# mLSTM scores of heads 1 to 3 from high and low parts, in three float32r products

## The chip, the cores and the metric

The program runs on one core of a Trainium2 chip. The metric is the device time of one execution in microseconds. The time before is 1564.88 us, the median of three runs (1564.79 to 1565.66).

## The reference

Two layers of a hybrid backbone over 512 latent and 256 context tokens of width 1024, all in float32. The even layer projects its input, runs a convolution group beside a bidirectional mLSTM group (4 heads of 128), and projects out; the odd layer has pooling and attention. A ConvFFN follows in each. The part that matters here is the chunkwise mLSTM:

```
s   = einsum('bhld,bhsd->bhls', qj, kj) * exp(dmat - m_t)
num = w_inter * einsum(qj, C) + einsum('bhls,bhse->bhle', s, vj)
den = w_inter * einsum(qj, n) + sum(s, -1)
h   = num / max(abs(den), exp(-m_t))
```

It is run forward and backward with separate gates, and the two results are added. q and k are used in full float32. The kernel computes the same without a carried state: all scores of a head, weighted by one exponential for each direction.

## The kernel before, in words

The layout puts channels on the 128 partitions and tokens on the free axis (T = 768: 512 latent, then 256 context). `qkov` holds 16 blocks of 128x768: queries of heads 0 to 3, keys of heads 0 to 3, values, and the output gates. `h_hi` and `h_lo` hold the two float32r parts of the layer's input (eight blocks of 128x768 each), which are not needed once the even projection is done; later they take the parts of the mixer's output.

The mLSTM stage works through the list `ITEMS` (L193): six score items ("S", head, q) for each head, q going over the key tiles in the order 4, 5, 0, 1, 2, 3 (`ORDER`, context tiles first), and from head 1 on one item "X" for the head before, which turns its normalised result. Each engine runs its own loop over the list, and semaphores couple them:

- PE (L1029): the score of item z goes to one of two PSUM slots. It waits until DVE has read the slot two items back. Then PE weighs the item before: probabilities times values (`weigh`, L1006), into PSUM sums of the head. So each score stands ahead of the weighing of its predecessor. Before the first weighing of a head, PE waits until the sums of the head before were read (`sums_taken_fwd`, `sums_taken_rev`).
- ACT (L1584): the exponentials of an item (`exps`, two or four, with four buffers that `p_used` frees), the squares of the head before at q 1 and 2, its square root at q 3 (two table loads), and the first two exponentials of the next head at q 5, then the copy of the reverse sums.
- POOL (L2595): a triangular mask on the diagonal block of each exponential.
- DVE (L2284): score times exponential (`weighted`, L2216), and in head 0 three reciprocals for the convolution's norm, in later heads the reverse sums, the norm factors, the convolution's norm; at the end of a head the merge of the head before, the first two products of the next head and `forward_sums` (L2230), which takes the denominators and reads the sums.

The order of the work on every engine is written out by hand in these loops. The score is one plain float32 matmul for each segment (L1045), with segments 0:512 and, for context tiles, also 512:768. Elsewhere in the kernel (L741, L790, L1166) a product is three float32r matmuls of parts: high x high, high x low, low x high. A high part is an ACT copy with rounding to float32r, a low part a DVE subtraction. `vt` (L1757) is the helper for every DVE tensor_tensor, so its instructions all have that line.

Of the kernel before, what the change touches and what calls it, by code (L numbers as in the profile page):

```python
# [28 lines left out]
F32 = mybir.dt.float32  # L29
F32R = mybir.dt.float32r  # L30
ALU = mybir.AluOpType
ACT = mybir.ActivationFunctionType
AX = mybir.AxisListType

P = 128
# [4 lines left out]
T = LAT + CTX  # L40
# [6 lines left out]
HEADS = 4  # L47
# [117 lines left out]
ORDER = (4, 5, 0, 1, 2, 3)  # L165
# [34 lines left out]
def build(nc, a, out):  # L200
# [3 lines left out]
    with ctx:  # L204
        used = {}

        def sem(name):
            if name not in used:
                used[name] = ctx.enter_context(nc.semaphore(name))
            return used[name]  # L210
# [6 lines left out]
        def place(name, shape, dt=F32, offset=None):  # L217

            size = int(np.prod(shape[1:])) * (2 if dt == mybir.dt.bfloat16 else 4)
            if offset is None:  # L220
                offset = at[0]
                at[0] += (size + 31) // 32 * 32
                assert at[0] <= top, (name, at[0] - top)
            assert offset + size <= top, name
            return nc.alloc_sbuf_tensor_at(name, shape, dt, offset=offset)
# [3 lines left out]
        h_hi = place("h_hi", [P, KD, T], F32R)  # L229
# [28 lines left out]


        qkov = place("qkov", [P, 16, T], offset=A0)  # L260
        negM = place("negM", [P, 2, 2, T], offset=A0 + 8 * T * 4)
        sig_b = place("sig_b", [P, 4, T], offset=A0 + 8 * T * 4)
        v_tok = place("v_tok", [P, NT, HEADS, VW], offset=A0 + 49152)
# [612 lines left out]
        def _(pe):  # L876
# [152 lines left out]
            for z, (kind, hd, q) in enumerate(ITEMS):  # L1029
                if z == 1:  # L1030
                    weigh(*pending)
                    pending = None
                if z >= 2:
                    was, of, q_ = ITEMS[z - 2]
                    if was == "S":
                        pe.wait_ge(sem("p_ready"), 16 * of + STEPS[q_][-1][0] + 1)
                    else:
                        pe.wait_ge(sem("merged_ready"), of + 1)
                elif not z:
                    pe.wait_ge(sem("conv_centred"), 4)  # L1040
                else:
                    pe.wait_ge(sem("ln_rooted"), 1)
                if kind == "S":
                    for t0, t1 in (SEGS[T] if ORDER[q] >= NL else SEGS[LAT]):
                        last = nc.tensor.matmul(acc[:, 1, z % 2, t0:t1], qkov[:, 4 + hd, ORDER[q] * P:(ORDER[q] + 1) * P],  # L1045
                                                qkov[:, hd, t0:t1], start=True, stop=True)
                else:
                    pe.wait_ge(sem("hn_ready"), hd + 1)
                    for j in range(NT):
                        last = transpose(acc[:, 1, z % 2, j * P:(j + 1) * P], h_tok[:, j, :])  # L1050
                last.then_inc(sem("slot_full"), 1)
                if kind == "S" and pending:
                    if pending[1] == 0 and hd:
                        pe.wait_ge(sem("sums_taken_fwd"), hd)
                        pe.wait_ge(sem("sums_taken_rev"), hd)
                    weigh(*pending)
                if kind == "S":
                    pending = (hd, q)
                if not z:
                    pe.wait_ge(sem("ln_sq_summed"), 1)  # L1060
                    for t0, t1 in SEGS[T]:
                        last = nc.tensor.matmul(acc[:, 1, 1, t0:t1], ones[:, :], ln_sq[0][:, t0:t1], start=True, stop=True)
                    last.then_inc(sem("ln_var"), 1)
                    psum_free(pe, U["mlstm"] + 1)
                if (kind, hd, q) == ("S", 0, 2):
                    last_columns()
# [180 lines left out]
        def _(act):  # L1247
# [11 lines left out]
            def unit_high(n, i=0):  # L1259

                take_high(n, i)
                take_high(n + 1, i)
# [316 lines left out]
            def head_out(hd):  # L1579

                act.wait_ge(sem("merged_ready"), hd + 1)
                nc.scalar.activation(h_hi[:, 4 + hd, :], merged[hd][:, :], ACT.Copy).then_inc(sem("mix_high"), 1)

            for kind, hd, q in ITEMS:  # L1584
                if kind == "S":
                    if hd or q:
                        exps(hd, q, 2 if not q else 0, 4)
                    if hd >= 2 and not q:
                        head_out(hd - 2)
                    if (hd, q) == (0, 0):  # L1590
                        conv_root()
                    if (hd, q) == (0, 1):
                        unit_high(G["o"] + 4)
                    if q in (1, 2) and hd:
                        head_squares(hd - 1, 3 * q - 3, 3 * q)
                    if q == 3 and hd:
                        head_root(hd - 1)
                    if q == 5:
                        if hd < HEADS - 1:
                            exps(hd + 1, 0, 0, 2)  # L1600
                        else:
                            conv_silu(0)
                        act.wait_ge(sem("den_read"), hd + 1)
                        nc.scalar.activation(h_rev[:, :, :].rearrange("p (b c) t -> p b c t", b=2), head_sums_of(1), ACT.Copy
                                             ).then_inc(sem("sums_taken_rev"), 1)
                        if hd == HEADS - 1:
                            head_out(hd - 1)
# [144 lines left out]
        def _(dve):  # L1752
# [3 lines left out]
            def vt(out_, in0, in1, op):  # L1756
                return nc.vector.tensor_tensor(out_, in0, in1, op)  # L1757

            def ada_sums(c, of, i=0, first=0, end=KD):

                seq, nv = c.seq, len(c.vectors)

                def used(k):
                    return 4 * seq + 5 + k // 2 + 4 * c.per_seq * i

                for k in range(first, end):
                    if k % 2 == 0:
                        dve.wait_ge(ada_full[k // 2], 16 * (seq + 1) + 16 * c.per_seq * i)
                    for e, x_ in enumerate(c.vectors):
                        w, scale = ada_w[:, k // 2, k % 2, :], cond[:, k, x_:x_ + 1]  # L1770
                        if not k:
                            ins = nc.vector.tensor_scalar(of[e], w, scale, None, ALU.mult)
                        else:
                            if k % 2 == 0:
                                dve.wait_ge(ada_used, used(k - 1))
                            else:
                                sd.wait(sd.value() - (nv - 1))
                            ins = nc.vector.scalar_tensor_tensor(of[e], w, scale, of[e], ALU.mult, ALU.add)
                        if k % 2 and e == nv - 1:
                            ins.then_inc(ada_used, 1)  # L1780
                        else:
                            sd.done(ins)
# [492 lines left out]
            def head_end(z, hd):  # L2275
# [3 lines left out]
                    weighted(z + 1, hd + 1, 0, 0, 2)  # L2279
                forward_sums(hd)  # L2280

            beside = [Chunk((0, 1), BESIDE["out0"][0] + e, 0, 0, 0) for e in range(2)]
            sums_e = sums_beside["out0"]
            for z, (kind, hd, q) in enumerate(ITEMS):  # L2284
                dve.wait_ge(sem("slot_full"), z + 1)
                if kind == "X":
                    nc.vector.scalar_tensor_tensor(merged[hd][:, :], acc[:, 1, z % 2, 0:T], vec0[:, 88 + hd:89 + hd],
                                                   qkov[:, 12 + hd, :], ALU.mult, ALU.mult).then_inc(sem("merged_ready"), 1)
                    head_end(z, hd + 1)
                    continue  # L2290
                weighted(z, hd, q, 2 if hd and not q else 0, 4)
                if hd == 0 and q in (2, 3, 4):
                    conv_inverse(256 * (q - 2))
                if (hd, q) == (0, 1):
                    unit_low(28)
                if q == 0 and hd:
                    reverse_sums(hd - 1)
                if q == 1 and hd >= 2:
                    head_low(hd - 2)
                if q == 2 and hd:  # L2300
                    head_inverse(hd - 1)
                if q == 4 and hd:
                    head_normed(hd - 1)
                if hd in (1, 2) and q in (2, 3):
                    conv_normed(2 * (hd - 1) + q - 2)
                if hd == HEADS - 1 and q in (1, 3):
                    ada_sums(beside[0], sums_e[0], first=q // 2, end=q // 2 + 1)
                if q == 5 and not hd:
                    head_end(z, hd)

# [345 lines left out]
```

## Time and profile before

| | |
|---|---|
| median of three runs | 1564.88 us |
| profiled execution, its own time | 1565.75 us |
| its span | 1564.0 us |
| granted TensorE clock | 0.999 |
| busy in the span: PE, PEld, DVE, ACT, POOL | 99%, 85%, 67%, 37%, 2% |
| mLSTM stage | first score at 269.70 us, first product of the output projection at 344.31 us |

The spans are microseconds from the start of one profiled execution. A busy PE is not a PE at its peak: matmuls overlap, so the time that one holds the engine is read from its start to the next one's start. A bracket behind an instruction tells how long its engine was idle before it and what ended that.

### The profile page before, as it was taken

How to read it: one execution, taken by the hardware profiler on the slowest of the kernel's cores; microseconds unless marked ns; L12 is line 12 of the kernel's file. 1: busy time of each engine (PE TensorE's matmuls, PEld its weight loads, DVE VectorE, ACT ScalarE, POOL GpSimd, SP SyncE). 2: the span in 40 equal slices, each digit the busy share in tenths (PEclk: the TensorE clock that was granted, in tenths of full speed). 3: DMA queues.
4: the chain of work that ended last, by engine and by line, in shares of the span. 5: the costliest groups of instructions: out<-in, count | busy, mean ns of one | idle time of the engine just before them, and what ended most of it. 6: DMA issues, size and time to landing. Idle time of an engine off the chain costs nothing. (4 is left out here: it accounts for less than half of the span.)

```text
span 1564.0 us, 21770 instructions
## 1 busy us (share of the span) xinstructions
PE 1544.2 (99%) x8590; PEld 1325.1 (85%) x8590; DVE 1047.2 (67%) x1567; ACT 572.4 (37%) x870; POOL 24.3 (2%) x66
## 2 busy tenths in 40 slices
PE   8999999999999999999999999998999999999998
PEld 5888888778898888888888888988988888888887
DVE  4999999888848784678626446877647543444346
ACT  5423224684722221122211225635646332322233
POOL 0000000220000000000000000000000000000000
PEclk9999999999999999999999999999999999999999
DMA  9632132125136453445333223340022323233232
GB/s 323 198 80 81 55 109 67 68 83 147 34 111 220 161 189 121 149 162 195 113 100 129 55 91 71 107 140 28 1 68 68 95 93 117 72 107 108 81 99 89
DMA packets 132746, 171.54 MB, mean 110 GB/s; under 512 B 16114, under 2 KB 88498, under 8 KB 132666
## 3 DMA queue, kind: packets, MB, share of 16 engines
q1 hardware_dynamic: 131770, 168.25, 33.7%
q0 software_dynamic: 640, 2.10, 0.3%
q8 instruction: 55, 0.90, 0.2%
q14 instruction: 25, 0.20, 0.0%
q10 hardware_dynamic: 256, 0.08, 0.0%
HBM read 166.17 MB, written 2.15 MB: 108 GB/s over the span
## 5 line engine op out<-in xcount | busy, mean ns | idle before, releaser
L741 PE MATMUL acc<-h_hi,w_hi 128*128 128x512 f32 (+1 forms) x1424 | 494.5, 351 | 0.0
L741 PE MATMUL acc<-h_lo,w_hi 128*128 128x512 f32 (+1 forms) x1424 | 492.4, 349 | 0.0
L741 PE MATMUL acc<-h_hi,w_lo 128*128 128x512 f32 (+1 forms) x1424 | 492.3, 349 | 0.0
L1757 DVE TENSOR_TENSOR w_lo<-raw,w_hi 128x1024 fp32r<-128x1024 f32 x183 | 218.1, 1219 | 131.9 <-ACT w_hi L1257 131.7
L741 PEld LDWEIGHTS acc<-h_hi,w_lo 128*128 128x128 f32 x1424 | 267.1, 189 | 35.0
L741 PEld LDWEIGHTS acc<-h_hi,w_hi 128*128 128x128 f32 x1424 | 267.3, 189 | 34.5
L741 PEld LDWEIGHTS acc<-h_lo,w_hi 128*128 128x128 f32 x1424 | 267.2, 189 | 33.8
L1257 ACT ACTIVATE w_hi<-raw 128x1024 fp32r<-128x1024 f32 x183 | 186.5, 1053 | 216.3 <-PE acc L790 150.7
L790 PE MATMUL acc<-w_hi,hid_hi 128*128 128x512 f32 x434 | 169.5, 391 | 0.0
L790 PE MATMUL acc<-w_hi,hid_lo 128*128 128x512 f32 x434 | 168.9, 389 | 0.0
L790 PE MATMUL acc<-w_lo,hid_hi 128*128 128x512 f32 x434 | 168.8, 389 | 0.0
L1633 ACT ACTIVATE gpad<-acc 128x1024 f32<-128x1024 f32 (+1 forms) x33 | 28.0, 885 | 211.2 <-PE acc L700 95.6
L2386 DVE TENSOR_SCALAR hid<-gpad,ffn_cw 128x512 f32 (+1 forms) x66 | 25.2, 438 | 112.0 <-ACT gpad L1633 111.6
L790 PEld LDWEIGHTS acc<-w_hi,hid_lo 128*128 128x128 f32 x434 | 81.5, 188 | 17.1
L790 PEld LDWEIGHTS acc<-w_lo,hid_hi 128*128 128x128 f32 x434 | 81.5, 188 | 16.7
L790 PEld LDWEIGHTS acc<-w_hi,hid_hi 128*128 128x128 f32 x434 | 81.5, 188 | 16.6
L2130 DVE SCALAR_TENSOR_TENSOR conv_u<-conv_u,dw_w 128x783 f32<-128x783 f32 x90 | 88.2, 1026 | 0.0
L1643 ACT ACTIVATE hid_hi<-hid (+2 forms) x22 | 28.0, 1274 | 145.1 <-DVE hid L1757 145.1
L2384 DVE SCALAR_TENSOR_TENSOR hid<-gpad,ffn_cw,hid 128x512 f32 (+3 forms) x132 | 77.5, 656 | 0.0
L1757 DVE TENSOR_TENSOR hid<-hid,acc 128x1024 f32 (+3 forms) x22 | 32.7, 1487 | 52.4 <-PE acc L741 51.8
L790 PE MATMUL acc<-w_hi,h_hi 128*128 128x512 f32 x160 | 63.5, 397 | 0.0
L790 PE MATMUL acc<-w_hi,h_lo 128*128 128x512 f32 x160 | 62.4, 390 | 0.0
(300 smaller groups left out, 2067.8 us busy)
## 6 DMA issues: line engine op xcount, KB each, us to landing
ada_w<-in_ada_w SPq DMA_DIRECT2D x96, 512.0 KB, 5.7
raw<-in_ffn_w_in SPq DMA_DIRECT2D x88, 512.0 KB, 3.6
raw<-in_ffn_w_out SPq DMA_DIRECT2D x44, 512.0 KB, 4.4
raw<-in_even_w_in SPq DMA_DIRECT2D x24, 512.0 KB, 4.5
ada<-in_ada_w SPq DMA_DIRECT2D x8, 1024.0 KB, 12.0
raw<-in_odd_w_in SPq DMA_DIRECT2D x12, 512.0 KB, 3.7
raw<-in_even_w_out SPq DMA_DIRECT2D x8, 512.0 KB, 5.9
raw<-in_odd_w_out SPq DMA_DIRECT2D x8, 512.0 KB, 4.0
```

The source lines that it names most:

```text
L741: last = nc.tensor.matmul(acc[:, s, m, t0:t1], w[:, slot, kk, c], x_[:, k, t0:t1], start=(k == 0 and q == 0), stop=(k == KD - 1 and q == 2))
L790: last = nc.tensor.matmul(tile_bank(name, a, j), x_[:, k, j * P:(j + 1) * P], w[:, m_ % 4, 2 * kk:2 * kk + 2, :].rearrange("p a c -> p (a ...
L1257: nc.scalar.activation(dst, raw[:, n % 2], ACT.Copy).then_inc(high, 1)
L1633: last = nc.scalar.activation(gpad[:, :, c:c + t1 - t0], acc[:, u % 2, :, t0:t1], ACT.Copy)
L1643: nc.scalar.activation(hid_hi[:, k, 0:tokens], hid[:, k, 0:tokens], ACT.Copy).then_inc(sem("hid_high"), 1)
L1757: return nc.vector.tensor_tensor(out_, in0, in1, op)
L2130: sd.done(nc.vector.scalar_tensor_tensor(dst, src, tap, dst, ALU.mult, ALU.add))
L2384: ins = nc.vector.scalar_tensor_tensor(dst, src, c, dst, ALU.mult, ALU.add)
L2386: ins = nc.vector.tensor_scalar(dst, src, c, None, ALU.mult)
```

## The change

The scores of heads 1 to 3 are computed from parts: keys high and low, queries high and low, in three float32r matmuls (keys high x queries high, keys low x queries high, keys high x queries low). Head 0 keeps its float32 scores. The parts are made one head ahead: ACT copies the next head's keys into `h_lo` after the exponentials of q 2 and its queries into `h_hi` after those of q 4; DVE subtracts at q 3 (keys) and q 5 (queries), in place in `qkov` (`qk_lo` is the same memory as float32r). PE waits for both before the first score of heads 1, 2 and 3. ACT's copy of the keys comes ahead of the squares of q 2; DVE's subtraction of the queries comes ahead of item X.

```diff
         qkov = place("qkov", [P, 16, T], offset=A0)
+        qk_lo = place("qk_lo", [P, 8, T], F32R, offset=A0)
...
                 if kind == "S":
+                    if hd and not q:
+                        pe.wait_ge(sem("qk_split"), 2 * hd)
                     for t0, t1 in (SEGS[T] if ORDER[q] >= NL else SEGS[LAT]):
-                        last = nc.tensor.matmul(acc[:, 1, z % 2, t0:t1], qkov[:, 4 + hd, ORDER[q] * P:(ORDER[q] + 1) * P],
-                                                qkov[:, hd, t0:t1], start=True, stop=True)
+                        c = slice(ORDER[q] * P, (ORDER[q] + 1) * P)
+                        if not hd:
+                            last = nc.tensor.matmul(acc[:, 1, z % 2, t0:t1], qkov[:, 4, c], qkov[:, 0, t0:t1], start=True, stop=True)
+                            continue
+                        for x_, (k_, q_) in enumerate(((h_lo[:, hd, c], h_hi), (qk_lo[:, 4 + hd, c], h_hi), (h_lo[:, hd, c], qk_lo))):
+                            last = nc.tensor.matmul(acc[:, 1, z % 2, t0:t1], k_, q_[:, hd, t0:t1], start=(x_ == 0), stop=(x_ == 2))
...
+            def keys_high(hd):
+                nc.scalar.activation(h_lo[:, hd, :], qkov[:, 4 + hd, :], ACT.Copy).then_inc(sem("qk_high"), 1)
+
+            def queries_high(hd):
+                nc.scalar.activation(h_hi[:, hd, :], qkov[:, hd, :], ACT.Copy).then_inc(sem("qk_high"), 1)
...
+                    if q == 2 and hd < HEADS - 1:
+                        keys_high(hd + 1)
+                    if q == 4 and hd < HEADS - 1:
+                        queries_high(hd + 1)
                     if q in (1, 2) and hd:
                         head_squares(hd - 1, 3 * q - 3, 3 * q)
...
+            def keys_low(hd):
+                dve.wait_ge(sem("qk_high"), 2 * hd - 1)
+                vt(qk_lo[:, 4 + hd, :], qkov[:, 4 + hd, :], h_lo[:, hd, :].bitcast(F32), ALU.subtract).then_inc(sem("qk_split"), 1)
+
+            def queries_low(hd):
+                dve.wait_ge(sem("qk_high"), 2 * hd)
+                vt(qk_lo[:, hd, :], qkov[:, hd, :], h_hi[:, hd, :].bitcast(F32), ALU.subtract).then_inc(sem("qk_split"), 1)
...
+                if q == 3 and hd < HEADS - 1:
+                    keys_low(hd + 1)
+                if q == 5 and hd < HEADS - 1:
+                    queries_low(hd + 1)
                 if q == 5 and not hd:
                     head_end(z, hd)
```

## Rows read from the trace of the kernel before

**Rows 1.** The page, busy us, share of the span, instructions.
```profile
PE 1544.2 (99%) x8590; PEld 1325.1 (85%) x8590; DVE 1047.2 (67%) x1567; ACT 572.4 (37%) x870; POOL 24.3 (2%) x66
```
**Rows 2.** Busy time by stretch: PE, PEld, DVE, ACT, POOL; clock, DMA.
```profile
281.20:292.05 10.85, 10.22 (x56) 7.06 (x55) 10.32 (x19) 4.68 (x9) 1.73 (x7) 1.00 0.08 18
292.05:310.74 18.69, 17.10 (x106) 13.03 (x107) 14.67 (x37) 13.62 (x34) 4.86 (x12) 1.00 0.13 48
...
329.23:344.30 15.07, 14.49 (x98) 11.57 (x98) 13.00 (x29) 14.49 (x34) 4.51 (x11) 1.00 0.07 24
344.30:370.00 25.70, 25.70 (x120) 21.40 (x119) 25.44 (x53) 15.46 (x34) 0.00 (x0) 1.00 0.59 143
```
**Rows 3.** Waits, 292.05 to 310.74: total us, times, longest.
```profile
DVE probs L2227 <- POOL probs L2604: 2.7, 2, 1.5
...
ACT probs L1523 <- PE acc L1013: 1.6, 3, 0.9
...
PE acc L1013 <- DVE probs L2227: 0.7, 1, 0.7
```
**Rows 4.** Timeline of PE: start us, us, instruction, count, idle before.
```profile
287.35 1.45 PE L1045 MATMUL acc<-qkov 128*128 128x512 f32 x4
288.64 1.49 PE L1013 MATMUL acc<-v_tok,probs 128*128 128x129 f32 x10
...
292.05 2.72 PE L1013 MATMUL acc<-v_tok,probs 128*128 128x129 f32 x22 [0.63 <-DVE h_tok L2252]
...
297.93 1.02 PE L1045 MATMUL acc<-qkov 128*128 128x512 f32 x2
298.79 1.28 PE L1013 MATMUL acc<-v_tok,probs 128*128 128x129 f32 x10
...
305.96 1.56 PE L1045 MATMUL acc<-qkov 128*128 128x512 f32 x4
```
**Rows 5.** Timeline of PE in the odd layer's attention.
```profile
1095.34 0.48 PE L1166 MATMUL acc<-k_hi,q_hi 128*128 128x512 f32 x1
1095.65 0.39 PE L1166 MATMUL acc<-k_hi,q_lo 128*128 128x512 f32 x1
...
1096.12 0.28 PE L1166 MATMUL acc<-k_hi,q_hi 128*128 128x256 f32 x1
...
1096.48 0.82 PE L881 MATMUL acc<-ident,ptile 128*128 128x128 f32 x6
```
**Rows 6.** Timeline of DVE at the end of head 0.
```profile
286.44 1.74 DVE L2192 RECIPROCAL ln_root<-ln_root 128x256 f32<-128x256 f32 x1
288.10 1.76 DVE L2227 SCALAR_TENSOR_TENSOR probs<-acc,probs 128x128 f32<-128x128 f32 x4
290.17 0.24 DVE L2240 SCALAR_TENSOR_TENSOR den<-acc,gcols 128x6 f32<-128x6 f32 x2 [0.31 <-PE acc L1013]
```
**Rows 7.** Timeline of ACT, head 1, tiles 4 and 5.
```profile
300.90 1.28 ACT L1523 ACT_TABLE_LOAD   x1
302.19 1.92 ACT L1523 ACTIVATE probs<-negM,gcols 128x256 f32<-128x256 f32 x4
304.46 1.24 ACT L1523 ACTIVATE probs<-negM,gcols 128x512 f32<-128x512 f32 x2 [0.34 <-PE acc L1013]
```
**Rows 8.** Timeline of DVE, head 1, tiles 4 and 5.
```profile
303.17 0.99 DVE L2227 SCALAR_TENSOR_TENSOR probs<-acc,probs 128x256 f32<-128x256 f32 x2 [1.49 <-POOL probs L2604]
...
304.94 0.96 DVE L2227 SCALAR_TENSOR_TENSOR probs<-acc,probs 128x128 f32<-128x128 f32 x2
```
**Rows 9.** Groups by form: count, busy us, mean ns, idle before.
```profile
L1582 ACT ACTIVATE h_hi<-merged 128x768 fp32r<-128x768 f32 x4 | 3.3, 836 | 5.9 <-DVE merged L2328 5.9
...
L1757 DVE TENSOR_TENSOR h_lo<-merged,h_hi 128x768 fp32r<-128x768 f32 x4 | 3.8, 949 | 0.0
```
**Rows 10.** Timeline of POOL: masks with and without a two-input multiply beside them.
```profile
304.18 1.00 POOL L2604 TENSOR_SCALAR_AFFINE_SELECT probs<-probs 128x128 f32<-128x128 f32 x1 [0.32 <-ACT probs L1523]
305.77 0.29 POOL L2604 TENSOR_SCALAR_AFFINE_SELECT probs<-probs 128x128 f32<-128x128 f32 x1 [0.59 <-ACT probs L1523]
```

## The prediction

> **What bounds the kernel now.** I read the page first. TensorE is busy for 99% of the span [rows 1], so a cheaper product looks like time won one for one. That is the average over the program. The change lies in one stage, the bidirectional mLSTM, from 269.7 us (first score) to 344.3 us (first product of the output projection), so I read the stretches there. In head 1's period, 292.05 to 310.74, PE counts 17.10 us of 18.69 as busy, DVE 14.67 and ACT 13.62 [rows 2]: no engine has the stage to itself. The waits of that period come next [rows 3]: DVE waits for a masked exponential, PE waits for DVE's weighted scores, ACT waits for probability buffers that PE frees. So there is a ring, score on PE, exponential on ACT, mask on POOL, product on DVE, weighing on PE, and at several points of each head its later members set the pace. The timelines [rows 4, 6, 7, 8] show where: the reader is to look for a bracket after an instruction (idle, and who ended it), and for instructions that follow each other with no bracket, which means a full engine. After 344.30 PE is busy for all of 25.70 us [rows 2]; whatever the mLSTM stage gains or loses arrives at the end in full.
>
> **Part 1, the scores (PE, removed and added).** A plain float32 score of a latent tile (128x512) holds PE from 297.93 to the next instruction's 298.79, 0.86 us; one of a context tile (512 and 256 columns) from 287.35 to 288.64, 1.29 us [rows 4]. The odd layer's attention already has scores in three float32r products of the same shape between float32 instructions: they start at 1095.34, the 256 part at 1096.12, the next instruction at 1096.48 [rows 5]. So 0.78 us and 1.14 us, savings of 0.08 and 0.15. A head has four latent and two context tiles: 0.62 us, and heads 1 to 3 together 1.86 us. This is the most that PE can give back.
>
> The Trainium skill ("FP8 and Floating Point Precision", TensorE Precision Notes) says that true FP32 takes four passes through the array; three passes of four would save 0.21 of the 0.86 us, 4.5 us in all for 18 512-wide and six 256-wide scores. The row gives less because the first product after float32 work takes 0.31 us to the next start (1095.34 to 1095.65 in the same timeline) and the others about 0.23. The sum goes by the row.
>
> **Part 2, the parts (ACT and DVE, added).** For each of heads 1, 2, 3: two ACT copies 128x768 into float32r and two DVE subtractions 128x768. The same forms are in the trace: 836 ns and 949 ns [rows 9]. Consecutive instructions of one engine overlap by 0.08 to 0.09 us (DVE: 286.44 + 1.74 is 288.18, the next starts at 288.10 [rows 6]; I take the same on ACT), so in a full queue one costs 0.75 us on ACT and 0.87 on DVE. Six of each: 4.5 us and 5.2 us of queue time. No DMA is issued, nothing is added on POOL. Whether they cost depends on the place.
>
> **Part 3, the wait.** PE waits for both parts before the first score of heads 1, 2, 3. Behind it on PE stands the last weighing of the head before, and for that wait DVE's denominators, the reading of the sums and the first weighing of the new head.
>
> *Head 0 to 1.* DVE is busy for 10.32 of 10.85 us here [rows 2]: three reciprocals of 1.74 us lie between the products (the last is shown), and its first idle time is 0.31 us before 290.17 [rows 6]. The four products at 288.10 are head 0's last tile (until about 288.99, 0.89 us for the 128 and 512 wide pair) and head 1's first two. Both keys_low (at tile 3) and queries_low (after tile 5) come ahead: 288.99 + 0.87 + 0.87 = 290.73, and 0.05 later, 290.78, PE may start a score that now starts at 287.35 [rows 4]. It takes 1.14, the weighing behind it 1.11 (ten instructions of 0.111) and its drain 0.17: 293.20. The denominators now start at 290.17, behind the same weighing. So they are 3.03 late, and with them the reading of the sums that releases PE at 292.05 [rows 4, 6]. DVE's first products of head 1 (0.89 us after the score ends at 292.1) are done at 293.0 and do not add. ACT's two copies here are hidden: it is busy for 4.68 us of that stretch [rows 2]. Term: +3.0. From below, if PE's own queue were the limit, 0.
>
> *Heads 1 to 2, and 2 to 3* (the two periods look alike, so I work out head 1's). ACT runs with no idle from 295.6 to 304.1: squares, exponentials, a table load, a root, a table load, then at 302.19 the four exponentials of tiles 4 and 5 [rows 7]. keys_high sits before this chain, so those four come 0.75 later; DVE's wait of 1.49 us before 303.17 [rows 8] now ends 0.75 later, and keys_low fits into it. queries_high falls among the four exponentials; tile 5's are needed by DVE only at 304.94 [rows 8], after head 0's normalising product, which itself moved by 0.75. Tile 5's second exponential ends at 304.11 [rows 7], with both copies 305.61; its product would start at 304.94 + 0.2 (the 128 wide one before it) + 0.75 = 305.89 at the earliest, and the mask between the two takes 0.29 [rows 10]. That leaves about 0.1. Then queries_low stands between tile 5's products, which end at 305.90 [rows 8], and the merge: 0.87 on the path, because PE's score of the next head started at 305.96 with that very end [rows 4]. The shorter score gives 0.15 back. Sum 0.75 + 0.10 + 0.87 - 0.15 = +1.57 a boundary, +3.1 for two. Bounds: -0.15 if the wait and the ACT chain had slack that I do not see; 2 x (0.75 + 0.87) - 0.15 = 3.1 each if both parts count in full.
>
> *Savings inside a head.* After the boundary PE goes straight into the weighing that frees ACT's buffers, then ACT's full chain sets tile 4, where PE waits (0.74 us, L1013 on DVE's products [rows 3]). A tile 1 to 3 score that is 0.08 shorter only makes that wait longer. I count 0; at most 0.47 (4 x 0.08 + 0.15) a head. Head 3 makes no parts, and its saving goes the same way.
>
> **Sum.** +3.0 + 3.1 + 0 = +6.1, I take +6.2 for the semaphore steps of two further handovers. The profiled execution took 1565.75 us (span 1564.0, 1.75 around it), which gives 1571.95; the median of the three runs is 0.87 below that execution, so the forecast is 1564.88 + 6.2 = 1571.1 us.
>
> **Rivals.**
> A. *PE is the bound and everything is hidden: faster.* Mechanism: the parts end before PE reaches the waiting score, so that the wait never decides and 0 to 1.86 us come off. It decides if DVE finishes head 0's tile 5 and both parts by 287.35. For it: 99% on PE [rows 1]. Against: at 287.35 DVE is still in a reciprocal that ends at 288.18, with tile 5's 0.89 us of products behind it [rows 6]. 1563.0 to 1564.9 us.
> B. *Only head 0 pays.* If the later heads' parts fall into waits, the first boundary's 3.0 remains, less 0.15 at each later one: about 1567.6 us. For it: DVE is idle for 4.0 us of the period and ACT for 5.1 [rows 2]. Against: ACT's idle time lies outside the chain before tile 4, and queries_low stands ahead of the merge, not in DVE's wait of 1.49.
> C. *The masks are held up by the subtractions.* POOL's select takes 0.29 us, but 1.00 us for the one at 304.18 [rows 10], when DVE is in a two-input multiply of 128x768, the normalising product between its rows at 303.17 and 304.94 [rows 8]. If keys_low lies over the select of tile 4, DVE's products are up to 0.7 later in heads 1 and 2: 1571.1 + 1.4 = 1572.5 us. Against: DVE is free from 301.68 (303.17 - 1.49), 302.43 with the shift, so keys_low ends at 303.3, before tile 4's first exponential does (302.19 + 0.75 + 0.5 = 303.4 [rows 7]).
> The Trainium skill states this rule ("SBUF — State Buffer", Who interferes with whom: a VectorE instruction with two SBUF inputs contends with a GpSimd instruction that reads SBUF); the trace agrees, 1.00 against 0.29 us.
> D. *All parts count in full*: 6 x (0.75 + 0.87) = 9.7, with the handovers +10: 1575 us.
>
> **How the numbers follow.** Forecast 0.70, A 0.03, B 0.12, C 0.10, D 0.05. The range goes from just under B's time to near D's, 1567.3 to 1574.3. A measurement tells about 0.2% (3.1 us) from no change, so slower starts at 1568.0: the forecast, C and D and a small part of B, 0.86; within 0.2%: most of B and some of A, 0.12; faster 0.02.
>
> **What would show it.** In the trace after: PE's first score of head 1 waits for DVE's subtraction, and starts 3.4 us later than 287.35, and head 1's own weighing starts at 295.1 instead of 292.05; the period from one release by the sums to the next grows from 18.69 to about 20.3; the third stretch, head 3, keeps its 15.1; DVE waits less than 1.49 before tile 4 of head 1, and the ACT copies show at about 0.84 us. The out0 projection starts at 350.5. The forecast is wrong if the first score of head 1 starts before 290, if head 1's period stays under 19, or if head 3's falls by over 0.5.

## The result, and the profile after

| | before | after |
|---|---|---|
| median, six runs each | 1565.04 us | 1572.36 us (1571.73 to 1573.12) |
| profiled execution, its own time | 1565.75 us | 1572.08 us |
| its span | 1564.0 us | 1570.3 us |
| mLSTM stage, first score to first product of the output projection | 74.61 us | 81.63 us |

The ratio is 1.0046, 95% interval 1.0035 to 1.0057: slower, by 7.3 us in the medians; 1571.1 was forecast. In the two profiled executions the stage is 7.02 us longer (350.52 - 268.89 against 344.31 - 269.70). After it both traces are alike: 1219.8 us to the end against 1219.7. Ahead of it the trace of the kernel before is 0.81 us the longer one (269.70 against 268.89), which is why the spans differ by 6.3 us only; that execution was 0.71 us over its median, the one of the change 0.28 under.

The page after. Its first line has the same meaning as [rows 1]: PE has about as much to do as before, in a longer span.

```profile
PE 1543.7 (98%) x8614; PEld 1329.9 (85%) x8614; DVE 1052.8 (67%) x1573; ACT 576.1 (37%) x876; POOL 23.8 (2%) x66
```

The stage, cut where PE is released by the reading of a head's sums (columns as in [rows 2]: length; busy time and instructions of PE, PEld, DVE, ACT, POOL; clock, DMA).

```profile
295.32:315.43 20.11, 16.33 (x114) 14.02 (x115) 16.39 (x38) 14.59 (x36) 4.62 (x12) 1.00 0.12 49
315.43:335.53 20.10, 16.34 (x114) 14.03 (x115) 17.24 (x39) 15.32 (x37) 4.62 (x12) 1.00 0.51 180
335.53:350.52 14.99, 13.99 (x102) 12.23 (x102) 13.06 (x29) 14.40 (x34) 4.20 (x11) 1.00 0.01 2
```

In head 1's period PE counts 0.77 us less busy time than before (16.33 against 17.10), DVE 1.72 and ACT 0.97 more, and the period grows by 1.42. What PE has to do did not set its length.

PE around the boundary from head 0 to head 1, to be read beside [rows 4] (start, duration, instruction, idle before):

```profile
284.46 1.02 PE L1050 MATMUL acc<-qkov 128*128 128x512 f32 x2
286.17 1.40 PE L1014 MATMUL acc<-v_tok,probs 128*128 128x129 f32 x10 [0.69 <-DVE probs L2244]
289.99 0.47 PE L1053 MATMUL acc<-h_hi,h_lo 128*128 128x512 f32 x1 [2.42 <-DVE qk_lo L1774]
290.30 0.39 PE L1053 MATMUL acc<-h_hi,qk_lo 128*128 128x512 f32 x1
...
291.12 2.28 PE L1014 MATMUL acc<-v_tok,probs 128*128 128x129 f32 x10
293.05 0.78 PE L1053 MATMUL acc<-h_hi,h_lo 128*128 128x512 f32 x1
293.62 0.63 PE L1053 MATMUL acc<-h_hi,qk_lo 128*128 128x512 f32 x1
...
295.32 2.72 PE L1014 MATMUL acc<-v_tok,probs 128*128 128x129 f32 x22 [0.26 <-DVE h_tok L2269]
```

Two things stand there. First, PE waits 2.42 us for DVE's subtraction; the first score takes 1.13 us (289.99 to 291.12), as worked out. Second, the ten weighing instructions behind it take 1.93 us (291.12 to 293.05). In the kernel before, the ten at this place took 1.33 (from 288.64 to the line below). And a 512-wide product lasts 0.63 us where the one at 290.30 lasted 0.39.

```profile
289.97 1.46 PE L1045 MATMUL acc<-qkov 128*128 128x512 f32 x4
```

The granted clock of PE in the changed kernel (columns: length, busy and instructions of PE, clock, DMA):

```profile
288.00:290.00 2.00, 0.01 (x1) 1.00 0.02 4
290.00:291.00 1.00, 1.00 (x5) 1.00 0.00 0
291.00:292.00 1.00, 1.00 (x8) 0.59 0.00 0
292.00:293.00 1.00, 1.00 (x7) 0.50 0.00 0
293.00:294.00 1.00, 1.00 (x4) 0.50 0.00 0
294.00:295.00 1.00, 1.00 (x5) 0.70 0.05 22
```

TensorE had been idle for 2.42 us up to 289.99 and for 0.69 us up to 286.17. It took up its work at 1.00, and then ran at 0.50, the level of 1.2 GHz, for 3.4 us (a stretch of 1 us at 0.59 has 0.82 us of it, the one at 0.70 has 0.60, and two are full). The trace of before has 1.00 over the same work.

DVE in the same execution, head 0's end and the later boundary (beside [rows 6, 8]):

```profile
286.51 1.74 DVE L2209 RECIPROCAL ln_root<-ln_root 128x256 f32<-128x256 f32 x1
288.17 0.81 DVE L2244 SCALAR_TENSOR_TENSOR probs<-acc,probs 128x128 f32<-128x128 f32 x2
288.90 0.94 DVE L1774 TENSOR_TENSOR qk_lo<-qkov,h_hi 128x768 fp32r<-128x768 f32 x1
291.32 1.02 DVE L2244 SCALAR_TENSOR_TENSOR probs<-acc,probs 128x512 f32<-128x512 f32 x2 [1.47 <-PE acc L1053]
...
305.47 0.95 DVE L1774 TENSOR_TENSOR qk_lo<-qkov,h_lo 128x768 fp32r<-128x768 f32 x1
307.08 0.99 DVE L2244 SCALAR_TENSOR_TENSOR probs<-acc,probs 128x256 f32<-128x256 f32 x2 [0.67 <-POOL probs L2633]
...
310.01 0.95 DVE L1774 TENSOR_TENSOR qk_lo<-qkov,h_hi 128x768 fp32r<-128x768 f32 x1
310.87 1.01 DVE L2312 SCALAR_TENSOR_TENSOR merged<-acc,vec,qkov 128x768 f32<-128x768 f32 x1
```

The reader is to see the keys' subtraction inside the wait before tile 4 (0.67 of the 1.49 us is left), and the queries' subtraction directly ahead of the merge, with PE waiting for it ahead of the first score of head 2:

```profile
311.10 0.47 PE L1053 MATMUL acc<-h_hi,h_lo 128*128 128x512 f32 x1 [1.16 <-DVE qk_lo L1774]
```

### The profile page after: what moved, and what is told of

Same layout as the page of the kernel before. It is cut to its first block and busy times, and to the rows that moved or that the text cites. A ratio compares the mean times of both kernels' runs of the same rounds, so it can differ in the third digit from the quotient of the medians.

```text
span 1570.3 us, 21833 instructions
## 1 busy us (share of the span) xinstructions
PE 1543.7 (98%) x8614; PEld 1329.9 (85%) x8614; DVE 1052.8 (67%) x1573; ACT 576.1 (37%) x876; POOL 23.8 (2%) x66
## 5 line engine op out<-in xcount | busy, mean ns | idle before, releaser
L2413 DVE SCALAR_TENSOR_TENSOR hid<-gpad,ffn_cw,hid 128x512 f32 (+3 forms) x132 | 77.6, 658 | 0.0
```

The costliest lines, as they stand in the source:

```text
L2413: ins = nc.vector.scalar_tensor_tensor(dst, src, c, dst, ALU.mult, ALU.add)
```

## The experiments

All were made from the changed kernel. The table cuts each profiled stage in four, in us: from the first score to the release by head 0's sums (the boundary 0 to 1), the two full periods of heads 1 and 2, and the rest with head 3. The last column is the median device time; a number in brackets is the number of executions, the others are one execution. The stages are each of one profiled execution. The kernel before had medians of 1564.99, 1565.07, 1565.10 and 1565.03 beside them.

| kernel | to head 1 | head 1 | head 2 | head 3 | stage | time |
|---|---|---|---|---|---|---|
| before | 22.35 | 18.69 | 18.49 | 15.08 | 74.61 | 1565.04 (6) |
| the change | 26.43 | 20.11 | 20.10 | 14.99 | 81.63 | 1572.36 (6) |
| e1 parts only | 23.67 | 19.49 | 19.49 | 15.07 | 77.72 | 1568.06 |
| e2 products only | 22.35 | 18.36 | 18.18 | 14.98 | 73.87 | 1564.35 (10) |
| e3 both, no wait | 23.68 | 19.27 | 19.28 | 14.99 | 77.22 | 1567.87 |
| e4 head 1 alone | 27.43 | 18.41 | 18.50 | 15.08 | 79.42 | 1569.85 |
| e5 heads 2 and 3 | 22.35 | 20.18 | 20.09 | 14.99 | 77.61 | 1569.44 |
| e6 change, PE kept busy | 25.36 | 20.10 | 20.10 | 14.99 | 80.55 | 1571.51 (4) |
| e7 change, keys copied earlier | 27.43 | 19.38 | 19.35 | 14.99 | 81.15 | 1572.82 |
| e8 heads 2 and 3, parts in waits | 22.36 | 18.27 | 18.60 | 14.98 | 74.21 | 1565.03 (10) |
| e9 float32, wait of head 1 | 25.67 | 19.49 | 19.50 | 15.08 | 79.74 | 1570.58 |
| e10 head 1 alone, PE kept busy | 25.36 | 18.42 | 18.49 | 15.08 | 77.35 | 1568.61 |
| e11 as e5 | 22.35 | 20.18 | 20.10 | 15.00 | 77.63 | 1568.34 (10) |
| e12 as e9 | 26.73 | 19.50 | 19.50 | 15.07 | 80.80 | 1572.16 (4) |

**e1, parts only.**

```diff
-                    if hd and not q:
-                        pe.wait_ge(sem("qk_split"), 2 * hd)
...
+                        last = nc.tensor.matmul(acc[:, 1, z % 2, t0:t1], qkov[:, 4 + hd, c], qkov[:, hd, t0:t1], start=True, stop=True)
+                        continue
...
-                vt(qk_lo[:, 4 + hd, :], qkov[:, 4 + hd, :], h_lo[:, hd, :].bitcast(F32), ALU.subtract)...
+                vt(h_lo[:, hd, :], qkov[:, 4 + hd, :], h_lo[:, hd, :].bitcast(F32), ALU.subtract)...
```

> The parts are made at the change's places, but every score stays the plain float32 one, PE does not wait for the parts, and the low parts are written over the high ones (nobody reads them). Stage = from the first score to the first product of the output projection: 74.61 us before, 81.63 after. Theory (full queues on DVE and ACT): the parts alone cost about 1.4 us at the boundary 0 to 1 and 0.9 at each of the next two, stage about 77.8 us (+3.2), and PE's clock does not fall. Rival 'it is the wait alone': stage within 0.5 us of 74.6. Rival 'the products': the same, 74.6.

Measured: +3.11 us in the stage: 1.32 at the first boundary, 0.80 and 1.00 in the next two periods, with no fall of the clock. The queue time of ACT and DVE alone has this price; it is less than half of the change's 7.0.

**e2, products only.**

```diff
-                        for x_, (k_, q_) in enumerate(((h_lo[:, hd, c], h_hi), (qk_lo[:, 4 + hd, c], h_hi), (h_lo[:, hd, c], qk_lo))):
+                        for x_, (k_, q_) in enumerate(((h_lo[:, 0, c], h_hi), (h_lo[:, 0, c], h_hi), (h_lo[:, 0, c], h_hi))):
...
-                    if q == 2 and hd < HEADS - 1:
-                        keys_high(hd + 1)
```

> The scores of heads 1 to 3 are three float32r products, of what lies in the first block of the two part buffers; no parts are made and PE waits for none (so the scores are not those of the reference). Theory (the ring sets the pace, not PE): only about 0.2 to 0.3 us of the 1.86 us of PE time come off the stage, 74.3 us, the whole within 0.5 us of before. Rival 'PE is the bound': 1.4 to 1.9 us come off, stage under 73.2. Rival 'the products cost by themselves' (float32r beside float32): stage over 75.

Measured: 0.74 us came off the stage, 1564.35 us, ratio 0.9996 (0.9987 to 1.0006). The ring gives the shorter score back for the most part, but not as fully as I expected: 0.33 and 0.31 a period. Of the 1.86 us that PE saves, 0.74 reach the end of the stage when no parts are made. That is the most that the products gained in any run here.

**e3, both, no wait.** The edits of e1 on the parts and of e2 on the products, without the wait.

> As the change, with parts and three products, but the products read the first block of the part buffers and PE does not wait for the parts (so the scores are not those of the reference). Theory: as parts alone, +3.2 us, stage 77.8 us, no idle of 2.4 us on PE ahead of head 1's first score and no fall of the clock; the other 3.8 us of the change's 7.0 are the three waits and what follows them. Rival 'queue time alone': stage still over 81.

Measured: stage +2.61, no idle time of 2.4 us and no fall of the clock. That is 0.50 under e1: the three products give this back even with the parts in the queues, 0.22 and 0.21 of it in the periods of heads 1 and 2. Against e3, the waits of the whole change cost 0.84 and 0.82 us at the later two boundaries (20.11 - 19.27, 20.10 - 19.28), the price of one subtraction in a full queue, and 2.75 us at the first, clock included.

**e4, head 1 alone.**

```diff
-                    if hd and not q:
-                        pe.wait_ge(sem("qk_split"), 2 * hd)
+                    if hd == 1 and not q:
+                        pe.wait_ge(sem("qk_split"), 2)
...
-                        if not hd:
+                        if hd != 1:
...
-                    if q == 2 and hd < HEADS - 1:
+                    if q == 2 and hd == 0:
```

> Parts and three products for head 1 alone; heads 0, 2, 3 keep the float32 score. Theory: the boundary 0 to 1 is the change's (+4.1 us with the fall of the clock), the later periods are those of before or up to 0.2 shorter; stage 74.6 + 4.0 = 78.6 us. Rival 'each head costs the same' (7.0 / 3): 77.0 us.

Measured: 79.42, 0.8 over the expectation. Head 2's period is that of before and head 1's is 0.28 shorter (18.41), a little more than expected; the first boundary is 27.43 and not 26.4. The clock fell earlier there, in the idle time, and stayed down for 6.8 us instead of 3.4 (read in the same way; 291 to 294 is at 0.50 too). Stretches of PE in e4 (columns: length, busy and instructions, clock):

```profile
288.00:290.00 2.00, 0.00 (x0) 0.74 0.02 4
290.00:291.00 1.00, 0.84 (x2) 0.50 0.00 0
...
294.00:295.00 1.00, 1.00 (x5) 0.50 0.00 0
295.00:296.00 1.00, 1.00 (x5) 0.61 0.00 0
296.00:297.00 1.00, 0.74 (x6) 1.00 0.86 350
```

**e5 and e11, heads 2 and 3 alone, one kernel run twice.**

```diff
-                        if not hd:
+                        if hd < 2:
...
-                if q == 3 and hd < HEADS - 1:
+                if q == 3 and hd in (1, 2):
```

> Parts and three products for heads 2 and 3; heads 0 and 1 keep the float32 score, so nothing is added in head 0. Theory: the two later boundaries are the change's, +1.4 and +1.6, no fall of the clock; stage 74.6 + 3.0 = 77.6 us. Rival 'each head costs the same' (2 x 7.0 / 3): 79.3 us.

> The kernel with heads 2 and 3 from parts once more, now timed in rounds: its stage was the predicted 77.61 us, but the whole was 4.4 us over before, 1.4 of it behind the stage. Theory (the 1.4 us belong to that one execution): the median lies 2.8 to 3.4 us over before. Rival (something behind the stage depends on when it ends): 4.2 us or more over before.

Measured: stages of 77.61 and 77.63, the expected 77.6, with the clock at 1.00. The single execution of e5 lost 1.4 us more behind the stage; in ten executions the median lies 3.24 us over before (ratio 1.0020, 1.0010 to 1.0029), so that loss is not the kernel's.

**e6, the change with PE kept busy.**

```diff
                 if kind == "S":
+                    if (hd, q) == (1, 0):
+                        for _ in range(10):
+                            nc.tensor.matmul(acc[:, 1, z % 2, 896:1024], ones[:, :], ones[:, :], start=True, stop=True)
                     if hd and not q:
```

> The change, with ten extra 128x128 float32 matmuls of ones into an unused part of the score's PSUM slot on PE ahead of the wait for head 1's parts; they fill 2.2 of the 2.4 us of idle time. Theory 'clock': the granted clock stays at 1.00 (it was 0.50 to 0.59 from 291 to 294 in the change), head 1's first weighing of the sums comes about 1.0 us earlier, and the stage takes 80.6 us, 1.0 less than the change. Rival 'DVE's queue': the clock is not the cause of the 1.05 us beyond the predicted boundary; the stage stays at 81.6, or is longer by what the extra matmuls take.

Measured: the extra matmuls fill the idle time, the clock stays at 1.00, and the weighing behind the first score takes 1.03 us (291.47 to 292.50) instead of 1.93. The timeline of PE in e6, where one float32 matmul is two instructions (the ten stand as x20):

```profile
287.82 2.40 PE L1047 MATMUL acc<-ones 128*128 128x128 f32 x20
290.31 0.50 PE L1056 MATMUL acc<-h_hi,h_lo 128*128 128x512 f32 x1
...
291.47 1.28 PE L1014 MATMUL acc<-v_tok,probs 128*128 128x129 f32 x10
292.50 0.48 PE L1056 MATMUL acc<-h_hi,h_lo 128*128 128x512 f32 x1
...
294.67 2.50 PE L1014 MATMUL acc<-v_tok,probs 128*128 128x129 f32 x20 [0.87 <-DVE h_tok L2272]
```

The boundary is 25.36, which is 3.01 over before, and the stage 1.08 shorter than the change's. So work that computes nothing made the stage shorter. For the whole time this is not shown: the medians are 1571.51 and 1572.36 us, but the runs overlap at their ends (1570.94 to 1571.92, and 1571.73 to 1573.12), they were made at different times, and beside the kernel before the two ratios have much the same interval (1.0026 to 1.0060, and 1.0035 to 1.0057). The mean clocks of e6's four executions are 0.999 or 1.000, those of the change's six 0.997 to 0.999.

**e10, head 1 alone with PE kept busy.** e4 with the edit of e6.

> Head 1 alone from parts, with the ten extra matmuls of ones ahead of its wait. Theory: the clock stays at 1.00; head 1's sums are taken 25.4 us after the first score, against 27.43 without the extra matmuls, where the clock was 0.50 from about 289.3 to 295.2; stage 77.4 us against 79.42. Rival 'the extra time of head 1 alone is not the clock': stage stays within 0.4 us of 79.4.

Measured: 25.36 and 77.35. So the longer stretch at 0.50 in e4 had cost 2.07 us, the shorter one in the change 1.07.

**e9 and e12, float32 scores with the wait of head 1, one kernel run twice.** e1 with one wait:

```diff
+                    if (hd, q) == (1, 0):
+                        pe.wait_ge(sem("qk_split"), 2)
```

> Every score is plain float32; the parts are made at the change's places (low parts written over the high ones, read by nobody), and PE waits for head 1's parts ahead of head 1's first score, and for no others. So PE's idle time of 2.4 us is there without a float32r product behind it. Theory 'idle time lowers the clock': the granted clock falls to 0.50 behind the idle time, as in the change; head 1's sums are taken 26.5 to 27.6 us after the first score (22.35 before, 23.67 with the parts and no wait). Rival 'float32r products in the scores lower it': clock 1.00 throughout, and 25.5 us (22.35 + 3.0 + 0.15 for the longer score).

> The kernel with float32 scores and PE's wait for head 1's parts once more, in about ten executions: in its first one the idle time of 2.42 us was there and the clock stayed at 1.00 (span 1568.9, mean clock 1.000). Theory 'the idle time lowers the clock, but not in every execution': some of the executions have a mean clock of 0.997 or 0.998 and are 1 to 2 us longer than the shortest (1569.5 to 1572.5), as those of the change (0.997 to 0.999). Rival 'it takes the float32r products behind the idle time': all executions have 0.999 or 1.000 and lie within 1 us of each other at 1570 to 1571.

Measured: in e9 the idle time of 2.42 us was there and the clock did not fall; that was against the theory as I had put it. e12 has the same idle time and the fall. First e9, then e12, PE's stretches:

```profile
290.00:292.00 2.00, 1.49 (x6) 1.00 0.00 0
292.00:294.00 2.00, 2.00 (x14) 1.00 0.00 0
```

```profile
290.00:292.00 2.00, 2.00 (x8) 0.81 0.00 0
292.00:294.00 2.00, 2.00 (x9) 0.50 0.00 0
294.00:296.00 2.00, 1.96 (x8) 0.84 0.58 235
```

The ten weighing instructions behind head 1's first score take 1.11 us in e9 and 2.14 in e12:

```profile
291.88 1.28 PE L1014 MATMUL acc<-v_tok,probs 128*128 128x129 f32 x10
292.99 1.45 PE L1049 MATMUL acc<-qkov 128*128 128x512 f32 x4
```

```profile
291.22 2.35 PE L1014 MATMUL acc<-v_tok,probs 128*128 128x129 f32 x10
293.36 2.09 PE L1049 MATMUL acc<-qkov 128*128 128x512 f32 x4
```

The two traces are of one kernel, with the fall and without it, and their first boundaries differ by 1.06 us (26.73 against 25.67), the rest of the stage by nothing. This is the price of the fall once more, without any extra matmuls.

The four executions of e12 took 1570.95, 1571.55, 1572.77 and 1572.78 us at mean clocks of 0.998, 0.999, 0.997 and 0.997. So the float32r products are not needed for the fall, and the idle time does not bring it in every execution. What decides between none, 1 and 2 us stays open. As the fall can be absent by itself, one trace of a kernel at 1.00 proves little; that the extra matmuls hold the clock rests on all five executions with them (e6, e10) having mean clocks of 0.999 or 1.000, against 0.997 to 0.999 in the eight of the change, e4 and e7.

**e7, the change with the keys of heads 2 and 3 copied earlier.**

```diff
-                    if q == 2 and hd < HEADS - 1:
-                        keys_high(hd + 1)
+                    if (hd, q) == (0, 2):
+                        keys_high(1)
...
                             exps(hd + 1, 0, 0, 2)
+                            if hd < HEADS - 2:
+                                keys_high(hd + 2)
```

> The change, with ACT's copy of the keys of heads 2 and 3 moved one head forward, to the end of the head before the last, behind the first exponentials, where ACT waits over 3 us for the denominators. Theory: the copy of 0.75 us leaves the full ACT chain ahead of tile 4, so the periods of heads 1 and 2 fall from 20.1 to 19.4 us each and the stage from 81.6 to 80.1. Rival 'only the subtraction and the wait on PE count': periods stay at 20.1, stage 81.6.

Measured: the periods are 19.38 and 19.35 (19.4 expected), 0.73 and 0.75 less, the effective length of one copy. The stage gained only 0.5, because in this execution the clock was down for the longer time (27.43 to head 1, as e4); with the change's 26.43 it would be 80.15. The copy's place was the cost.

**e8, heads 2 and 3, every part in a wait.**

```diff
                             exps(hd + 1, 0, 0, 2)
+                            if hd < HEADS - 2:
+                                keys_high(hd + 2)
+                                queries_high(hd + 2)
...
-                if q == 5 and hd < HEADS - 1:
-                    queries_low(hd + 1)
+                if q == 2 - hd % 2 and hd in (1, 2):
+                    queries_low(hd + 1)
+                if q == 3 and hd in (1, 2):
+                    keys_low(hd + 1)
```

> Parts and three products for heads 2 and 3, each piece in a wait: both ACT copies at the end of the head before the last, in ACT's wait for the denominators; DVE's subtraction of the queries at tile 1 (head 1) or 2 (head 2) position of the list, that of the keys at position 3, both ahead of DVE's wait before tile 4. Theory (place, not amount, is the cost): stage 74.3 to 75.2 us, against 77.6 for the same two heads in the change's places; the time is that of before within 0.1%. Rival 'amount': 3.5 us of DVE and 3.0 of ACT work cost at least half of the +3.0, stage over 76.

Measured: 74.21, and 1565.03 us against 1565.07 (ratio 1.000, 0.999 to 1.001). The same instructions for the same two heads cost 3.0 us of stage in e5, and here the stage is 0.40 shorter than before. The copies on ACT lie where ACT waited for the denominators before (first line, the kernel before, 3.43 us), and 1.74 us of that wait are left (the other lines, e8 at head 1's end):

```profile
309.13 0.81 ACT L1604 ACTIVATE h_rev<-acc 128x768 f32<-128x768 f32 x1 [3.43 <-DVE den L1757]
```

```profile
304.98 0.83 ACT L1592 ACTIVATE h_lo<-qkov 128x768 fp32r<-128x768 f32 x1
305.71 0.83 ACT L1595 ACTIVATE h_hi<-qkov 128x768 fp32r<-128x768 f32 x1
308.28 0.81 ACT L1620 ACTIVATE h_rev<-acc 128x768 f32<-128x768 f32 x1 [1.74 <-DVE den L1773]
```

DVE's subtraction of the queries (295.82) and of the keys (300.98), each followed by a product that still waits for its mask:

```profile
295.82 0.95 DVE L1773 TENSOR_TENSOR qk_lo<-qkov,h_hi 128x768 fp32r<-128x768 f32 x1
297.13 0.89 DVE L2243 SCALAR_TENSOR_TENSOR probs<-acc,probs 128x512 f32<-128x512 f32 x2 [0.36 <-POOL probs L2632]
...
300.98 0.95 DVE L1773 TENSOR_TENSOR qk_lo<-qkov,h_lo 128x768 fp32r<-128x768 f32 x1
302.54 0.99 DVE L2243 SCALAR_TENSOR_TENSOR probs<-acc,probs 128x256 f32<-128x256 f32 x2 [0.61 <-POOL probs L2632]
```

In head 2's period the placed work is not all hidden: it takes 18.60 us, 0.11 over before and 0.42 over e2, where the products stand alone. Head 1's period is 0.42 shorter than before, which no run takes apart. So for heads 2 and 3 placing makes the change free, not fast: e2 shows 0.7 us to win with all three heads. A placing of head 1's parts, whose boundary costs most, was not tried. No kernel here beats the kernel before by more than a measurement tells.

## Why the prediction was right, point by point

- *The scores (0.78 and 1.14 us).* Right: the first context tile takes 1.13 us (289.99 to 291.12), and the latent tile that starts at 297.80 is followed by a weighing at 298.58, 0.78 us later.
- *The parts (0.84 and 0.95 us alone, 0.75 and 0.87 in a full queue).* Right: the wait for one subtraction cost 0.84 and 0.82 (change against e3), the copy of the keys 0.73 and 0.75 (e7).
- *The boundary 0 to 1, +3.0.* Its mechanism, place and size hold: PE's first score of head 1 came 3.45 us later relative to the stage (21.10 us after the first score, 17.65 before; 3.43 worked out), and with PE kept busy the boundary is 3.01 longer (e6, e10; 3.03 worked out). By the runs, 1.32 of it is queue time alone (e1) and the rest comes with the wait (25.36 - 23.68 = 1.68, e6 against e3). What I left out stands on top: the fall of TensorE's clock, 1.07 us in the profiled execution. I had counted the wait and not asked what the clock does behind it.
- *The later boundaries, +1.57 each.* Measured +1.42 and +1.61. For head 1: e7 shows 0.73 for the keys' copy, the change against e3 0.84 for the queries' subtraction, and what is given back is 0.33 (e2 against before) or 0.22 (e3 against e1), not my 0.15. That leaves 1.42 - 0.73 - 0.84 + 0.33 = 0.18, or 0.07, for the queries' copy, where I had 0.10; this last one is a remainder, not a run of its own.
- *Savings inside a head, 0.* Nearly: head 3's stretch is 0.09 shorter, and head 1 alone has 0.28 (e4). It was a term at its lower bound.
- *Sum.* 3.0 + 3.1 forecast, 4.08 + 3.03 - 0.09 = 7.02 measured in the stage. Of this 1.07 is the clock. The other 5.95 us lie 0.15 under the +6.1: the two later boundaries are 0.11 smaller than worked out, and head 3 gives back 0.09.
- *The output projection at 350.5.* It started at 350.52, but by luck: the stage began 0.81 us earlier than in the trace of before and was 0.82 longer than its old length and the 6.2 give. The time is to be compared by the stage, 81.63 us against 80.8.
- *Rivals.* A falls: e2 wins 0.74 us of PE's 1.86 without any part, so PE was not the bound. B falls: e5 has both later boundaries in full. By the time alone C (1572.5) lies nearest to the measured 1572.36, but its cause is not there: the mask of tile 4 took 0.29 us at 306.69, after the subtraction had ended at 306.42. D falls by the two later boundaries together (3.03 and not 6.2) and by e8.

The Trainium skill's rule on two SBUF inputs ("SBUF — State Buffer", Who interferes with whom) was weighed for C. The trace after agrees with it where it applies: of the two masks from 308.22 on, beside DVE's normalising product of 308.00 to 308.95, both together take 1.12 us, and the mask at 309.85 takes 0.29. In head 0 a mask that started at 285.45, beside the keys' subtraction of 284.89 to 285.79, took 0.48 us; so C's mechanism touched a mask there, but DVE's products follow the subtraction without a bracket.

```profile
285.45 0.48 POOL L2633 TENSOR_SCALAR_AFFINE_SELECT probs<-probs 128x128 f32<-128x128 f32 x1 [0.48 <-ACT probs L1530]
...
306.69 0.29 POOL L2633 TENSOR_SCALAR_AFFINE_SELECT probs<-probs 128x128 f32<-128x128 f32 x1 [2.72 <-ACT probs L1530]
...
308.22 1.12 POOL L2633 TENSOR_SCALAR_AFFINE_SELECT probs<-probs 128x128 f32<-128x128 f32 x2 [0.73 <-ACT probs L1530]
309.85 0.29 POOL L2633 TENSOR_SCALAR_AFFINE_SELECT probs<-probs 128x128 f32<-128x128 f32 x1 [0.51 <-ACT probs L1530]
```

## What to carry to other kernels

An engine that is busy for 99% of the program can be off the critical path in the very stage that a change touches; read the waits of that stage before counting what its instructions save. Preparatory work costs by its place: ask of each added instruction whether it stands in its engine's wait or ahead of what others wait for. And where a change adds a wait on TensorE like the 2.42 us here, look at the granted clock behind it: its fall had a price of its own, 1.07 or 2.07 us on top of the wait.

## What the runs showed of the hardware that I had not expected

An idle time of 2.42 us on TensorE, behind a stretch in which it had already waited 0.69 us, was followed by full work at a granted clock of 0.50, the level of 1.2 GHz, for 3.4 us (the change) or 6.8 us (e4, e7, part of it still idle), at a cost of 1.07 and 2.07 us (change and e4, against e6 and e10); with ten matmuls of ones in the gap it stayed at 1.00 in both kernels tried (e6, e10). In e9 the same idle time was followed by no fall, and in e12, the same kernel, by one of 3.4 us that cost 1.06. The fall began either inside the idle time (e4, 288 to 290 at 0.74; e7 likewise) or more than a microsecond after PE had work again (the change, e12). Idle times of 1.16 us at the later boundaries were followed by none: PE's clock is 1.00 over the periods of heads 1 and 2 in the change, e5, e6, e7 and e11.
